# Another order of the chain between output projection and up-projection, and one low weight part made by POOL

## What is computed

```
mix = merge_branches(...) @ w_out
x = x + RMSNorm_post(mix)
u = RMSNorm_pre2(x) @ w_ffn_up          # 1024 -> 2 * 2816
c = conv_b + causal width-3 convolution of u
f = (gelu(c[..., :D_FF]) * c[..., D_FF:]) @ w_ffn_down
x = x + RMSNorm_post2(f)
```

## Time and profile before

| | |
|---|---|
| median of 3 runs | 1010.09 us |
| the runs | 1008.38 to 1010.45 us |
| the profiled execution | 1009.0 us, span 1007.2 us |
| TensorE busy | 985.4 us, 98% of the span |
| VectorE, ScalarE, POOL busy | 55%, 38%, 18% |
| chain that ended last | PE 91%, DVE 4%, DMA 2% |
| mean granted clock of TensorE | 0.997 |

### The profile page before, as it was taken

The page is one execution under the profiler, slowest core; times in us unless marked ns, Lnnn a source line. Parts: engine busy times, 40 slices in busy tenths (PEclk is TensorE's granted clock), DMA queues, the critical chain, the costliest instruction groups (busy, mean ns, idle before and its releaser), DMA issues.

```text
span 1007.2 us, 20394 instructions
## 1 busy us (share of the span) xinstructions
PE 985.4 (98%) x7774; PEld 876.2 (87%) x7774; DVE 551.8 (55%) x912; ACT 378.6 (38%) x832; POOL 180.1 (18%) x365
## 2 busy tenths in 40 slices
PE   5999999999999999999999999999999999999997
PEld 4788788779999899999887789999999999777775
DVE  5354125535367877783145677666666666422225
ACT  6333232441543333333133644444444444212413
POOL 2102004034162343445100001000000000000100
PEclk9999999999999999999999999999999999999999
DMA  6734545546796676769635324555545553221323
GB/s 243 267 137 160 175 160 169 190 154 216 254 295 222 217 226 195 225 202 330 207 102 173 109 77 168 178 178 174 176 166 176 172 189 128 85 84 64 121 84 118
DMA packets 40466, 175.36 MB, mean 174 GB/s; under 512 B 6937, under 2 KB 7385, under 8 KB 38865
## 3 DMA queue, kind: packets, MB, share of 16 engines
q1 hardware_dynamic: 25616, 125.78, 36.2%
q0 software_dynamic: 14784, 48.65, 15.1%
HBM read 164.40 MB, written 54.05 MB: 217 GB/s over the span
## 4 chain that ended last, share of the span: by engine, by line
PE 91%; DVE 4%; DMA 2%; ACT 1%; issue 1%; SPq 0%; DVEq 0%; POOL 0%; ACTq 0%
PE bank L1339 11%; PE bank L1340 10%; PE bank L1341 10%; PE bank L1857 9%; PE bank L1858 9%; PE bank L1859 9%; PE bank L1421 6%; PE bank L1427 6%; PE bank L1426 6%; PE bank L1358 3%; PE bank L1321 2%; DMA wraw<-in_weights 1%; PE bank L1756 1%; PE bank L1762 1%; PE bank L1761 1%
## 5 line engine op out<-in xcount | busy, mean ns | idle before, releaser
L1942 DVE TENSOR_TENSOR wlo<-wraw,whi 128x1024 fp32r<-128x1024 f32 x88 | 107.6, 1222 | 277.5 <-ACT whi L839 277.1
L839 ACT ACTIVATE whi<-wraw 128x1024 fp32r<-128x1024 f32 x90 | 95.3, 1059 | 318.1 <-PE bank L1341 208.4
L1857 PE MATMUL bank<-T1h,whi 128*128 128x288 f32 (+1 forms) x704 | 202.4, 288 | 1.8 <-DVE T1l L1952 1.6
L1858 PE MATMUL bank<-T1l,whi 128*128 128x288 f32 (+1 forms) x704 | 203.6, 289 | 0.0
L1859 PE MATMUL bank<-T1h,wlo 128*128 128x288 f32 (+1 forms) x704 | 203.2, 289 | 0.0
L1857 PEld LDWEIGHTS bank<-T1h,whi 128*128 128x128 f32 x704 | 133.0, 189 | 2.2 <-issue 1.8
L1858 PEld LDWEIGHTS bank<-T1l,whi 128*128 128x128 f32 x704 | 132.7, 189 | 0.0
L1859 PEld LDWEIGHTS bank<-T1h,wlo 128*128 128x128 f32 x704 | 132.3, 188 | 0.0
L1339 PE MATMUL bank<-whi,T1h 128*128 128x512 f32 (+1 forms) x288 | 113.8, 395 | 0.5 <-DVE T1l L1952 0.3
L1421 PE MATMUL bank<-T1h,whi 128*128 128x272 f32 x384 | 113.4, 295 | 0.0
L1427 PE MATMUL bank<-T1h,wlo 128*128 128x272 f32 x384 | 111.0, 289 | 0.0
(11 more groups left out here) (302 smaller groups left out, 1818.1 us busy)
## 6 DMA issues: line engine op xcount, KB each, us to landing
wraw<-in_weights SPq DMA_DIRECT2D x142, 512.0 KB, 3.7
out_s_kv_g<-in_cache_kv_g SPq DMA_DIRECT2D x64, 511.0 KB
qbc<-sample_queries POOLq DMA_DIRECT2D x48, 256.0 KB, 4.9
kvk<-in_cache_kv_g POOLq DMA_DIRECT2D x32, 256.0 KB, 4.3
kvv<-in_cache_kv_g POOLq DMA_DIRECT2D x16, 512.0 KB, 8.2
out_s_kv_g<-in_cache_kv_g SPq DMA_DIRECT2D x16, 508.0 KB
S<-in_state_ret POOLq DMA_DIRECT2D x16, 256.0 KB, 3.3
out_s_ret<-S POOLq DMA_DIRECT2D x16, 256.0 KB, 6.0
```

The costliest lines, as they stand in the source:

```text
L839: nc.scalar.activation(w_halves(s)[0], wraw[:, s % 2, :], ACT.Copy).then_inc(w_hi, 1)
L1857: mm(dst, Wh, T1h[:, k, c], start=k == 0, stop=False)
L1858: mm(dst, Wh, T1l[:, k, c], start=False, stop=False)
L1942: v.tensor_tensor(lo, wraw[:, s % 2, :], hi.bitcast(F), ALU.subtract).then_inc(w_lo, 1)
```

## The change

1. **Start, ScalarE:** `w_split(1)` is issued at `i == 3` in place of `i == 2`. POOL's second low part follows it.
2. **VectorE's chain:** all five `first_gain` come ahead of `w_split(S_UP)`; the first half of `hidden_lo(0)` comes ahead of `mixed(2)`; `hidden_scale(4)` comes ahead of `hidden_lo(3)`. ScalarE's `hidden_root(4)` comes ahead of `hidden_hi(3)`. `mixed` waits for counts of `x_gain` that fit.
3. **`w_split(S_UP + 1)` leaves VectorE**; POOL makes that low part, behind its DMA of the convolution's state.
4. **TensorE:** the first turn stands ahead of step 2 of `out_rows(3)` in place of step 1; the last tile's turn moves from behind `up_half(1, 0)` into it, one half ahead of k-step 4 and one ahead of k-step 6; `up_half(0, 1)` waits for the last tile's halves one by one, at k-steps 0 and 4.

```diff
+        pool.wait_ge(w_hi, S_UP + 2)
+        pool.wait_ge(w_lo, S_UP + 1)
+        nc.gpsimd.tensor_tensor(wlo[:, (S_UP + 1) % 2, :], wraw[:, (S_UP + 1) % 2, :], whi[:, (S_UP + 1) % 2, :].bitcast(F),
+                                ALU.subtract).then_inc(w_lo, 1)
         filled(pool, ("h2", NORM_ORDER[-1], 1))
...
-            if i == 2:
+            if i == 3:
                 w_split(1)
...
         mixed_root(4)
+        hidden_root(4)
         hidden_hi(3)
-        hidden_root(4)
         hidden_hi(4)
...
-        out_rows(3, {1: 0, 3: 1})
+        out_rows(3, {2: 0, 3: 1})
...
+        def last_turned(k):
+            if k in (4, 6):
+                turn_hidden(TILES - 1, (k // 2 - 2,))
+
+        def last_head(k):
+            if k % 4 == 0:
+                emptied(pe, ("h2", NORM_ORDER[TILES - 1], k // 4))
...
         pe.wait_ge(w_lo, S_UP + 2)
-        up_half(1, 0)
-        turn_hidden(TILES - 1)
+        up_half(1, 0, last_turned)
...
-        head_ready_for(TILES - 1)
-        up_half(0, 1).then_inc(w_used, 1)
+        up_half(0, 1, last_head).then_inc(w_used, 1)
...
+        for i in range(TILES):
+            first_gain(i)
         w_split(S_UP)
-        first_gain(0)
-        first_gain(4)
         second_gain(0)
-        first_gain(1)
         mixed(0)
...
         hidden_scale(1)
+        hidden_lo(0, (0,))
         mixed(2)
-        hidden_lo(0)
-        first_gain(2)
-        first_gain(3)
+        hidden_lo(0, (1,))
         hidden_lo(1)
...
-        w_split(S_UP + 1)
         hidden_scale(3)
         second_gain(4)
         mixed(4)
+        hidden_scale(4)
         hidden_lo(3)
-        hidden_scale(4)
         hidden_lo(4)
```

More of the change, by code:

```diff
@@ L1818, in _, with turn_hidden @@
         out_step(3)
-        def turn_hidden(p):
+        def turn_hidden(p, halves=(0, 1)):
             i = NORM_ORDER[p]
-            for half in range(2):
+            for half in halves:
                 pe.wait_ge(h_ready, 2 * p + half + 1)
@@ L1845, in _, with up_half @@
         out_rows(2, {})
-        out_rows(3, {1: 0, 3: 1})
+        out_rows(3, {2: 0, 3: 1})
         out_rows(4, {2: 2})
-        def up_half(j, half):
+        def up_half(j, half, amid=None):
             at_, width = UP_HALVES[half]
@@ L1854, in up_half @@
             for k in range(KT):
+                if amid:
+                    amid(k)
                 cut = slice(128 * k, 128 * k + 128)
@@ L2337, in mixed @@
                 dve.wait_ge(b_free[i], BLK_OUT + 2)
-            dve.wait_ge(x_gain, (1, 4, 4, 6, 6)[p])
+            dve.wait_ge(x_gain, TILES + 1 if p else TILES)
             for half in range(2):
@@ L2354, in hidden_scale, with hidden_lo @@
                 v.scalar_tensor_tensor(hn[0:r, p % 2, c], xo[0:r, i, c], rs, gffn[0:r, c], ALU.mult, ALU.mult).then_inc(h_ready, 1)
-        def hidden_lo(p):
-            for half in range(2):
+        def hidden_lo(p, halves=(0, 1)):
+            for half in halves:
                 split_evac(("h2", NORM_ORDER[p], half), T1h, T1l, 4 * half, NORM_ORDER[p])
```

## The result

| | before | after |
|---|---|---|
| median | 1009.97 us | 1011.82 us |
| the runs (20 each, in turns on the same chips) | 1007.81 to 1011.43 | 1010.59 to 1014.46 |
| ratio | | 1.0025, 95% interval 1.0017 to 1.0032 |
| the profiled execution | 1009.0 us, span 1007.2 | 1012.09 us, span 1010.3 |
| mean granted clock of TensorE, mean of the runs | 0.9974 (35 runs in the session of e1 to e4) | 0.9955 (20 runs) |

The changed kernel is slower by 2.5 us (1.7 to 3.2). The forecast was no change, which the interval excludes.

What follows compares the result with a forecast made beforehand. TensorE, busy 98% of the span, was taken as the bound, so only its work and idle places count. Transition -0.3 and start +0.5 gave +0.2 us, put on the median 1010.1: 1010.3 us, range 1007.9 to 1012.0.

Steps and rivals of the forecast that it cites:

- The transition: Around the first up-projection: the reordered chain and turns, with POOL's subtraction between the halves of `hn`, gain 0.3 us.
- The rival without exclusion: Transition: POOL's operand reads slip between VectorE's; with the start's 0.25, in all 2.7 us faster, 1007.4; chance 0.09.
- the two about POOL's place: POOL after both halves of `hn`: 0.7 us faster, 1009.4, chance 0.25; POOL before `hn`: 0.6 slower, 1010.7, chance 0.13.
- The reading rule behind this: VectorE and POOL: two instructions that both read two SBUF tensors exclude each other; whoever came first finishes.
- The start of the kernel: Start: the later weight split lets POOL hold the last `xn`; 0.5 us loss, bounds 0.25 gain and 0.5 loss.
- The clock as a rival: Pause inside `up_half(1, 0)`: idle PE drops to the low clock, costing 1.7 us; 1.9 slower, 1012.0; chance 0.13.
- the signs of being wrong that the prediction names: No VectorE instruction stretched by POOL, PE's clock falling behind the pause, or PE waiting at a place behind 607.

Runs made afterwards that it cites:

- e1: The kernel before with only the start's edit, ScalarE's second weight split at i == 3 in place of i == 2: 1012.47 us, ratio 1.0025.
- e4: e2 without POOL's subtraction; VectorE makes that low part ahead of `hn` of the fourth tile, as in before: 1008.17 us, ratio 0.9985.
- e5: e2 with POOL's subtraction waiting until both halves of `hn` of the fourth tile are written: 1009.12 us, ratio 1.0000.
- e2: The changed kernel with the start's edit undone, `w_split(1)` back at i == 2: 1010.45 us, ratio 1.0001 to before.
- e6: e2 without POOL's subtraction; ScalarE's copy and VectorE's subtraction for slot S_UP + 1 made early: 1006.11 us, ratio 0.9974.
- e9: e2 with 16 extra matmuls of 288 columns in PE's pause inside `up_half(1, 0)`: 1008.60 us, ratio 0.9999.
- e8: e1 with slot 1's low part made by VectorE behind the last `T1l` in place of POOL: 1011.70 us, ratio 1.0019.
- e3: The changed kernel with eight extra matmuls ahead of the start's last turn, results unused: 1010.19 us, ratio 1.0004 to before.

## Why the prediction was wrong

**What held.** The transition went as forecast, step by step. Less the 3.3 us by which after runs late there, the second half of the second turn is at 583.72 - 3.3 = 580.4 (580.4 forecast), `up_half(0, 0)` at 589.1 (589.05), POOL's subtraction at 590.0 (589.9), the last turn at 597.9 (597.8), after a wait of 2.69 (2.7), `up_half(0, 1)` at 600.4 (600.3). POOL got in between the two halves of `hn`. The stretch gives 0.2 (603.70 - 3.27 against 600.61), where 0.3 was forecast. The rival without exclusion is out (one VectorE pair is stretched by 2.14 us in every profile with the subtraction and no extra wait), and so are the two about POOL's place, of which e5 shows one by force. The reading rule behind this, that who comes first finishes, was taken from the earlier trace rows; the Trainium skill (SBUF — State Buffer, Who interferes with whom) has it as a lock for the whole instruction. The traces agree: the second half of `hn` ends at 596.43, 0.56 us behind POOL's end at 595.87, so nearly all of its own 0.7 us ran after POOL was done.

**What failed: the step "The start of the kernel".** Its term was +0.5 with bounds of -0.25 and +0.5, and it measured +2.9. Its mechanism was right: the fourth `xn` free, the split behind the third tile's evacuation, the last `xn` held by POOL (1.98 us, 1.9 forecast). Three things were missed in it.
1. The evacuation of the third tile. The step let it end at 17.0, from the trace of before. It ended at 18.2, because PE's turn of that tile came later: everything was 0.20 later at 13.37 already, and the loads at 14.82 and 15.25 were still slow. Before's profile was a lucky execution: the five kernels with the same start as before (e2, e4, e5, e6, e9) load at 13.47 to 13.61 what before loads at 13.17, and reach the start's mark at 24.41 to 24.70, not 24.00. In before's order the fourth turn waited 1.26 us for `xn`, which covered such a delay: in e4 the products behind the third turn begin as late as 17.58, that wait shrinks to 0.28, and the mark is at 24.51 all the same. With the split behind the evacuation it has no cover: split, square, `xn` and turn all move with it.
2. The interval in which PE stands still. The step moved the matmul at 22.44 by 0.5 and did not ask how long PE would now be idle ahead of it. It is 2.01 us, where before had 0.37.
3. What follows such an idle time. With the clock held, e1 reaches the mark at 25.17, which is 0.5 to 0.8 behind the 24.41 to 24.70 of the kernels with the old start. That is the forecast term. The rest is the clock: e8 and after, in which it fell, are at 26.03 and 26.86.

So over many executions the start costs about 0.6 from the edit itself and, by the mean clocks, 1.9 from the clock (0.9974 - 0.9955, times 1007 us; the 0.9974 is from another session, as the runs of before in the result have no clock on record). Their sum, 2.5, less the 0.2 of the transition, is 2.3, and the two means of the result (1012.24 and 1009.63) are 2.6 apart. Runs with the same clock show the other part alone: at 0.996 after has 1011.84 on average (9 runs) and before 1011.43 (7 runs, session of e1 to e4), 0.4 more, which fits the 0.6 of the edit less the 0.2 of the transition.

**The clock as a rival.** It was named with a chance of 0.13, a price of 1.7 us and a result of 1012.0. The price is nearly right (a whole fall costs 1.5). That the median of 1011.8 is close to the result is luck, since the rival was placed at the pause in `up_half(1, 0)`. There the clock held in after's profile (1.00 from 575 to 615). It fell there in the profiles of e2 and e3, which have the same pause of 2.70, one of the signs of being wrong that the prediction names; but e2, which has this pause without the start's wait, is at 1.0001, so it doesn't carry the loss. The argument against it, that the old wait of 1.78 us cost nothing, came from one execution; e1's profile shows the same wait with a fall behind it. So the mechanism of the rival is real, and the prediction went wrong in asking it of one idle interval only, when the change makes two: the term of the start has no clock in it.

The Trainium skill (TensorE: Matmul & The Clock Gate, HAM oscillation) tells of waits for data that bring the array back to the low clock. The traces agree that it happens, behind waits of 1.2 us and more (1.19 in e8 at 350, 2.70 in e2 at 598), and add that the same wait does it in one execution and not in the next.

## What to carry to other kernels

A reordering is judged by the longest stretch in which TensorE now stands still, not only by when its next matmul comes: at 98% busy, a wait of 1 to 3 us may cost 1.2 to 1.5 us of clock on top of itself. A profile of one execution shows one draw of this, so a term at such a wait needs a range of one fall up. If the start hangs on when full clock comes, ask which wait would hide a delay and whether the edit removes it. Handing an instruction to POOL cost VectorE more than it took off here (2.14 against 1.22 us), where both work from SBUF at the same time; e6 found it a hole in VectorE's own order instead.

## What the runs showed of the hardware

**The same wait lets the clock fall in one execution and not in another.** Behind the wait at 350 us, which none of the edits touches, the clock fell in before and not in e6, although e6 had waited longer. Before, then e6 (weight load, and windows of TensorE):

```profile
350.02 0.20 PEld L1609 LDWEIGHTS bank<-pT,av 128*64 128x64 f32 x4 [1.28 <-DVE stat L2172]
```

```profile
350.00:358.00 8.00, 7.98 (x76) 0.79 0.79 274
```

```profile
350.83 0.20 PEld L1609 LDWEIGHTS bank<-pT,av 128*64 128x64 f32 x4 [1.53 <-DVE stat L2180]
```

```profile
350.00:358.00 8.00, 7.17 (x81) 1.00 0.80 253
```

**The run times come in steps of it.** Sorted by the granted clock that came with each run, the means of before in one session are 1008.15 to 1008.34 us at 0.999 and 1.0, 1009.8 at 0.997 and 0.998, and 1011.4 at 0.995 and 0.996: steps of 1.6 us, about the price of one fall. e6 has 1005.6 at 1.0 and 1007.3 at 0.998. Most of the 3 us by which runs of one kernel differ is this. What decides in a single execution whether the clock falls is left open; the length of the wait alone does not. One difference stands out at the start: in after and e8, where it fell, the turn of the third tile began at the low level and the first load of 0.19 us behind it is at 17.24 and 17.22; in e1, where it held over the same 2.01 us, that turn was at full clock and the load is at 16.82. With three profiles this is a lead and no more.
